# Attention with signed scale in the queries, its output split where it is copied, scores two pairs ahead, and a rebuilt seam between two model blocks

## The reference, cut to what matters

```python
def chunk_causal_attention(q, k, v, scale):          # head size 96 for q and k, 64 for v
    ...
        s = jnp.einsum('bqhd,bkhd->bhqk', qi, k).astype(jnp.float32) * scale
        s = jnp.where(mask[None, None], s, NEG)
        p = jax.nn.softmax(s, axis=-1).astype(v.dtype)
        return jnp.einsum('bhqk,bkhd->bqhd', p, v)
...
    y_a = jnp.einsum('bse,ed->bsd', o_a.reshape(b, s, MLA_HEADS * MLA_V), w_o_a)
    o_b = indexed_sparse_attention(q_b, k_b, v_b, q_i, k_i, w_i * (IDX_HEADS ** -0.5), top_k)
    y_b = jnp.einsum('bse,ed->bsd', o_b.reshape(b, s, DSA_HEADS * DSA_HEAD_DIM), w_o_b)
```

```python
    return x + m.reshape(b, s, d)                     # end of the first block: m is the experts' output
    x = rmsnorm(x, final_norm_g)
    h = layer_norm(jnp.concatenate([meta, x], axis=1), ln_in_g, ln_in_b)   # 16 meta tokens in front
    p = h @ w_in[l]                                   # second block; its first columns are conv_in
```

## Time and profile before

| | us |
|---|---|
| median of 3 runs | 2207.22 (2206.83 to 2208.47) |
| the profiled execution | 2207.27, span 2205.5 |
| attention (`attend`), first scores to last value product | 307.9 to 421.75 |
| wait of PE up to the projection's first matmul | to 426.98 |
| seam: last matmul of the experts to first of conv_in | 869.9 to 910.72 |
| PE busy | 1984.2 (90% of the span) |
| DVE, ACT, POOL busy | 1306.4, 938.7, 708.1 |

### The profile page before, as it was taken

The page is one execution under the profiler, slowest core; times in us unless marked ns, Lnnn a source line. Parts: engine busy times, 40 slices in busy tenths (PEclk is TensorE's granted clock), DMA queues, the critical chain, the costliest instruction groups (busy, mean ns, idle before and its releaser), DMA issues. The chain is left out here.

```text
span 2205.5 us, 36863 instructions
## 1 busy us (share of the span) xinstructions
PE 1984.2 (90%) x14734; PEld 1680.3 (76%) x14734; DVE 1306.4 (59%) x1946; ACT 938.7 (43%) x1485; POOL 708.1 (32%) x378
## 2 busy tenths in 40 slices
PE   7999998799799997598999796688899979999997
PEld 4777744475687876598999576687689979999784
DVE  2769645541789897505999565566431167887402
ACT  4324248623688887522222543234333143333312
POOL 3433300141011111143443164321035425555441
PEclk9999989999799999699999898799789999999999
DMA  4222210021999998223223013210132212232221
GB/s 177 96 67 94 69 48 1 23 89 70 362 358 373 369 371 317 79 88 119 92 87 136 29 43 106 44 31 15 40 116 87 87 48 96 87 97 92 81 96 38
DMA packets 89378, 260.09 MB, mean 118 GB/s; under 512 B 26304, under 2 KB 27472, under 8 KB 88464
## 3 DMA queue, kind: packets, MB, share of 16 engines
q1 hardware_dynamic: 85488, 247.90, 31.9%
q0 software_dynamic: 3744, 10.11, 1.3%
HBM read 239.10 MB, written 18.87 MB: 117 GB/s over the span
## 5 line engine op out<-in xcount | busy, mean ns | idle before, releaser
L1546 DVE TENSOR_TENSOR moe_wlo<-moe_ring,moe_whi 128x1024 fp32r<-128x1024 f32 x198 | 233.0, 1221 | 39.9 <-ACT moe_whi L1542 39.0
L537 PE MATMUL acc<-h_xhi,h_whi 128*128 128x264 f32 x816 | 234.4, 287 | 13.3 <-DVE h_xlo L463 7.4
L537 PE MATMUL acc<-h_xlo,h_whi 128*128 128x264 f32 x816 | 233.4, 286 | 0.0
L537 PE MATMUL acc<-h_xhi,h_wlo 128*128 128x264 f32 x816 | 233.1, 286 | 0.0
L1542 ACT ACTIVATE moe_whi<-moe_ring 128x1024 fp32r<-128x1024 f32 x198 | 206.0, 1059 | 40.6 <-PE acc L1602 22.6
L537 PE MATMUL acc<-ff_xhi,ff_whi 128*128 128x258 f32 x704 | 200.9, 285 | 9.3 <-DVE ff_xlo L463 9.3
L537 PE MATMUL acc<-ff_xhi,ff_wlo 128*128 128x258 f32 x704 | 199.8, 284 | 0.0
L537 PE MATMUL acc<-ff_xlo,ff_whi 128*128 128x258 f32 x704 | 199.7, 284 | 0.0
L395 POOL TENSOR_TENSOR h_wlo<-ring,h_whi 128x1024 fp32r<-128x1024 f32 x49 | 117.5, 2400 | 201.4 <-ACT h_whi L387 201.4
L537 PEld LDWEIGHTS acc<-h_xhi,h_whi 128*128 128x128 f32 x816 | 155.9, 191 | 14.5 <-DVE h_xlo L463 8.5
L1987 DVE SCALAR_TENSOR_TENSOR acc<-cp,par,acc 128x528 f32<-128x528 f32 x232 | 159.2, 765 | 0.0
(11 more groups left out here) (506 smaller groups left out, 5131.6 us busy)
## 6 DMA issues: line engine op xcount, KB each, us to landing
ring<-slabs SPq DMA_DIRECT2D x213, 512.0 KB, 3.5
moe_ring<-moe_slabs SPq DMA_DIRECT2D x204, 512.0 KB, 6.1
tok_rows<-h_tok SPq DMA_DIRECT2D x5, 512.0 KB, 4.2
h_spill<-x2r SPq DMA_DIRECT2D x1, 2112.0 KB, 6.6
v_spill<-rw_v SPq DMA_DIRECT2D x1, 2112.0 KB, 7.4
y_spill<-cp SPq DMA_DIRECT2D x8, 264.0 KB, 4.5
rw_v<-v_spill SPq DMA_DIRECT2D x1, 2112.0 KB, 8.0
x2r<-h_spill SPq DMA_DIRECT2D x1, 2112.0 KB, 8.5
```

Of the source, the lines that this page charges most:

```text
L537: mm = nc.tensor.matmul(acc[j][0:rows, s, 0:t1 - t0], wp[:, at:at + rows], xp[:, t0:t1], start=(k == 0 and m == 0), stop=(k == kt - 1 and ...
L1546: tensor_tensor(wlo[u % AHEAD][:, :], ringm[u % RAW][:, :], whi[u % AHEAD][:, :].bitcast(F32), ALU.subtract).then_inc(w_lo[u % 2], 1)
```

## The change

In attention: the scale moves, with a minus sign, into the copies that make the queries; masks are positive instead of negative; DVE keeps the minimum, which is the exponential's bias as it stands (scale -1), so L1284 is gone. The two output copies become one of 128x128, which writes the rounded half straight into the projection's operand; DVE writes the rest from PSUM in a new step (`low`); the next stage has no roundings and rests of its own. `att_sc` has three buffers, scores and masks run two pairs ahead, and DVE scales p before it masks p+2.

In the seam: meta rows and gain are loaded during the experts' stage; ACT and POOL split conv_in's first two slabs during the seam, not ACT and DVE behind it; the product with the gain goes to a buffer of its own (`y`), so it doesn't wait for the sum of squares; only the small eps term (`easing`) waits.

```diff
-                            nc.scalar.activation(dests[i], acc[i % 4][0:rows, 0, :], ACT.Copy).then_inc(tile_out, 1)
+                            nc.scalar.activation(dests[i], acc[i % 4][0:rows, 0, :], ACT.Copy,
+                                                 scale=-HD ** -0.5 if KR < i <= KR + 4 else 1.0).then_inc(tile_out, 1)
...
-                sc = [[sbt(ax, f"att_sc{i}{h_}", [P, T1]) for h_ in two] for i in two]
+                sc = [[sbt(ax, f"att_sc{i}{h_}", [P, T1]) for h_ in two] for i in range(3)]
...
                     scores(0)
+                    scores(1)
                     for p in range(NP + 1):
-                        if p + 1 < NP:
-                            scores(p + 1)
+                        if p + 2 < NP:
+                            scores(p + 2)
                         if p >= 1:
                             values(p - 1)
                         if p < NP:
...
-                            nc.vector.tensor_tensor_reduce(scr(p, h_), sbank(p, h_), bias(pairs[p][1]), 1.0, -3e38,
-                                                           ALU.add, ALU.max, one(mx, p, h_)).then_inc(s_out, 1)
+                            nc.vector.tensor_tensor_reduce(scr(p, h_), sbank(p, h_), bias(pairs[p][1]), 1.0, 3e38,
+                                                           ALU.add, ALU.min, one(mn, p, h_)).then_inc(s_out, 1)
...
+                    def low(p):
+                        o = pairs[p][0][4]
+                        dve.wait_ge(o_hi, p + 1)
+                        nc.vector.tensor_tensor(to(p, o.lo), obank(p), to(p, o.hi).bitcast(F32), ALU.subtract).then_inc(o_lo, 1)
+
                     add_bias(0)
+                    add_bias(1)
                     for p in range(NP):
-                        if p + 1 < NP:
-                            add_bias(p + 1)
                         normal(p)
+                        if p + 2 < NP:
+                            add_bias(p + 2)
+                        if p >= 2:
+                            low(p - 2)
+                    low(NP - 2)
+                    low(NP - 1)
...
                             act.wait_ge(s_out, 2 * p + h_ + 1)
-                            link("act", act, nc.scalar.activation(one(nm, p, h_), one(mx, p, h_), ACT.Copy, scale=-scale))
-                            nc.scalar.activation(scr(p, h_), scr(p, h_), ACT.Exp, bias=one(nm, p, h_),
-                                                 scale=scale, accum_out=one(rs, p, h_)).then_inc(probs, 1)
+                            nc.scalar.activation(scr(p, h_), scr(p, h_), ACT.Exp, bias=one(mn, p, h_),
+                                                 scale=-1.0, accum_out=one(rs, p, h_)).then_inc(probs, 1)
...
-                    def store(p):
-                        o, qt, i = pairs[p][0][5], pairs[p][1], pairs[p][2]
-                        for h_ in two:
-                            act.wait_ge(o_ready, 2 * p + 2)
-                            nc.scalar.activation(o[64 * h_:64 * h_ + 64, i, qt * P:(qt + 1) * P], obank(p, h_),
-                                                 ACT.Copy).then_inc(o_out, 1)
+                    def high(p):
+                        act.wait_ge(o_ready, p + 1)
+                        nc.scalar.activation(to(p, pairs[p][0][4].hi), obank(p), ACT.Copy).then_inc(o_hi, 1)
...
-                    w.begin(act, ["w_o_a"], ax, bx)
...
-                    ax.dve(dve)
-                    bx.dve(dve)
...
+                def for_seam(sp):
+                    sp.dma_start(gain, final_row.to_broadcast([P, D])).then_inc(gain_in, 16)
+                    sp.dma_start(xm, meta_rows).then_inc(meta_in, 16)
...
                     nc.clear_and_free_semaphores(first_sems)
+                    for n in first_slabs:
+                        w.pool(pool, n)
...
                     nc.scalar.activation(dummy[:, :], k0("eps", 1, EPS_RMS), ACT.Sqrt)
+                    for n in first_slabs:
+                        w.act(act, n)
                     act.wait_ge(m_centred, 1)
...
                         v.tensor_tensor(x[t][:, :], x[t][:, :], x1[:, t, :], ALU.add).then_inc(added, 1)
+                        dve.wait_ge(added, t + 1)
+                        L(v.tensor_tensor_reduce(y[t][:, :], x[t][:, :], gain, 1.0, 0.0, ALU.mult, ALU.add, one(total, t)))
+                        v.tensor_scalar(one(minus, t), one(total, t), -1.0 / D, None, ALU.mult).then_inc(gained, 1)
+
+                    def easing(t):
                         dve.wait_ge(squared, t + 1)
-                        L(v.tensor_tensor_reduce(x[t][:, :], x[t][:, :], gain[:, :], 1.0, 0.0, ALU.mult, ALU.add, one(total, t)))
...
-                        w.act(act, first_slabs[0])
                         nc.scalar.activation(hx.hi[:, :, 0:META], h[:, :, 0:META], ACT.Copy).then_inc(meta_hi, 1)
-                        for q in range(4):
-                            round_turned(q)
-                        w.act(act, first_slabs[1])
-                        for q in range(4, KD):
+                        for q in range(KD):
                             round_turned(q)
...
-                        w.dve(dve, first_slabs[0])
...
-                            if q == 4:
-                                w.dve(dve, first_slabs[1])
```

140 lines of the change are left out of this document (74 added, 66 removed).

## The result

The changed kernel takes **2158.16 us** (median of 4 runs, 2157.65 to 2159.13), the kernel before 2207.02 on the same chip (2199.84 to 2208.47). The ratio is 0.9781, with a 95% interval of 0.9764 to 0.9798: 48.9 us less.

The account below looks back on a forecast made before the run. The prediction took the attention to be bound by a once-a-round ring set by queue order, with no engine full. Terms of 20.9, 4.5 and 6.6 sum to 32.0 us off 2207.27: 2175.3, forecast 2175, range 2164 to 2190.

Parts of the forecast that it names:

- term 1: Attention: cutting the ring leaves the engine with most work setting each round; 93.0 us against 113.85, 20.9 less.
- two half-clock stretches: Attention: PE at half clock again at the start and later, each shorter, costing about 4 and 2.5 us.
- the start has nearly the same wait: Attention start: PE waits nearly as long as before, so half clock returns there; ten us of it cost about 4.
- a rival of 0.12: Attention: no half clock at all, 6.5 us less and the seam's 1.4, total 2167; chance 0.12.
- the ring: Attention: transposes, scores, masks and scaling follow each other once a round, 4.31 us at 512 keys of the second kind.
- Term 2: Hand-over from attention to projection: first matmul 3.6 us behind ACT's slab copy, 2.9 less, plus 1.6 of clock: 4.5 less.
- Term 3: Seam and behind it: adds 3.6 us apart, net 2.45, and 4.3 behind the seam: 6.6 us less.
- The 0.3 us by which POOL or DVE comes first: Seam: POOL's second split starts 0.3 us before DVE's meta-row scaling, which waits; the first add is 1.4 us later.
- The low clock: Rival, attention: half clock lasts as long as now, 20 and 7 us; total 2181; chance 0.2.
- Hand-offs: Rival, attention: ACT, DVE and PE nearly equal at 512 keys, so waits cost 0.3 a round, 9.6 us: 2185; chance 0.18.
- the ring isn't cut: Rival, attention: masks still wait for buffers or banks, only the borders gain: 2196; chance 0.02.
- POOL didn't hold the last rest: Judges the rival at both borders: POOL holds the last rest (2.3 us) and the seam's first add (2.3): 2180; chance 0.1.

Follow-up runs that it names:

- only the ring back: Changed kernel with attention order and depth as before (masks ahead of scaling, one pair ahead, two score buffers): 2191.75 us.
- after at half clock: Changed kernel with the seam undone (first two conv_in slabs split in the next stage again), same attention; profiled execution had half clock: median 2162.1 us.
- after run again: The changed kernel itself, unchanged, with five more executions: 2158.52 us.
- faster version: Changed kernel with the projection's first slab copied and split at pair 14, and the seam's second slab copy and POOL split later: 2147.75 us.
- the seam alone: Changed kernel with only the seam's part of the faster version (second slab copied behind the meta rows' root, POOL's second split later): 2160.06 us.

## Why the prediction was wrong in size

**The mechanism of term 1 held, two sizes didn't.** The attention gave 34.7 us and not 20.9. The missing 13.8 are three pieces. Those of the rounds are in every trace of after's attention; that of the clock is in part luck.

*The clock, 6.5.* I had charged two half-clock stretches, 4 us at the start and 2.5 behind it; the profiled execution had none. The second stretch is gone by the change: from 340 to the end of the attention all ten traces with the scaling ahead of the masks are at full clock, and all four with the masks first have one (PEclk of 366 to 386: 0.83, 0.61, 0.77, 0.66). The first is in part luck: with after's own wait it came in two traces of six. The price itself was right: where it did come, it cost 5.9 us for 13.7 us of half clock, against my 4 for ten. What failed is the step "the start has nearly the same wait": PE waited 2.29 us there before and 0.53 after. I counted the third set of scores as evidence only for a rival of 0.12 and didn't work out what it does to the wait: 0.66 us of work (1.79 against 1.13) more, and 1.09 less until the transposes start, since the 128x1 operations no longer stand ahead of the first exponentials (with them back, the transposes started 3.41 us behind the first scores, as before; with only the ring back, 2.32, as in after).

*The rounds, 6.3.* By groups of four pairs (transposes to transposes, in us; the last group three rounds):

| keys, kind | before | forecast | after | after at half clock |
|---|---|---|---|---|
| 128, first | 12.3 | 7.3 | 6.3 | 11.1 |
| 256, first | 14.4 | 8.9 | 9.4 | 10.5 |
| 384, first | 15.4 | 12.0 | 12.9 | 12.9 |
| 512, first | 14.8 | 16.0 | 12.3 | 12.3 |
| 128, second | 10.0 | 7.3 | 5.5 | 5.5 |
| 256, second | 13.2 | 8.9 | 8.1 | 8.1 |
| 384, second | 15.4 | 10.6 | 10.5 | 10.5 |
| 512, second | 12.0 | 9.3 | 8.8 | 8.8 |

Two steps are mis-sized. The rounds at 512 keys of the first kind were put at 3.99, with their own scores of 1.81 in each. Two pairs ahead, three of the four rounds of that group carry scores of the next one, which has 128 keys: they took 2.85, bound by the ring of transposes, copy and values, and the heavy scores stand in rounds at 384 keys (3.33 each instead of 3.0) that paid less for them. That group gave 3.6 us over the forecast; the two groups at 256 and 384 keys of the first kind gave 1.4 less than it. A round has to be added up from what stands in it after the change, not from the work of its own pair. My own table should have warned me: 16.0 is more than the 14.8 of before. The second is at 128 keys, 2.8 us in the two groups. I put these rounds at DVE's sum, 1.82; they took 1.5 to 1.6 in the first kind and 1.4 to 1.5 in the second, though PE, ACT and DVE are all nearly full there (timeline of after, a stretch of ACT and one of DVE):

```profile
312.59 0.44 ACT L1322 ACTIVATE att_pt<-acc 128x128 f32<-128x128 f32 x2
...
312.91 0.41 ACT L1314 ACTIVATE att_sc<-att_sc,att_mn 128x128 f32<-128x128 f32 x1
...
313.29 0.41 ACT L1314 ACTIVATE att_sc<-att_sc,att_mn 128x128 f32<-128x128 f32 x1
```
```profile
352.60 0.29 DVE L1284 CUSTOM_DVE_ANT_0 att_sc<-acc,c 128x128 f32<-128x128 f32 x1 [0.68 <-PE acc L1241]
...
353.62 0.16 DVE L1290 RECIPROCAL att_ri<-att_rs 128x1 f32<-128x1 f32 x1
353.81 0.29 DVE L1291 TENSOR_SCALAR att_sc<-att_sc,att_ri 128x128 f32<-128x128 f32 x1
...
354.05 0.42 DVE L1284 CUSTOM_DVE_ANT_0 att_sc<-acc,sel 128x256 f32<-128x256 f32 x1
```

Two copies take 0.44 together, not 0.54, and the next exponential starts 0.38 behind the last, though each is 0.41 long and has a reading of 0.19 behind it: instructions that follow each other on ACT overlap here by about 0.1 us. On DVE the nine instructions from 352.60 on add up to 1.90 us, and the next round's first starts 1.45 behind. (For ACT I had left out the two readings of 0.19 a round; its sum of 1.61 came out right at 128 keys of the first kind because the overlap made up for them.) A sum of mean durations was here an upper end of DVE's round; the distance from start to start is the size to add up.

*The start, 1.0:* transposes begin 2.3 us behind the first scores; I had put 3.2 there (the trace of before has 3.41), and the end took 2.9 of 3.0.

**Term 2** was about right in the profiled execution: 2.96 of 2.9 for the hand-over (3.53 of 3.6 from the slab copy), and 1.1 of 1.6 for the clock, whose low stretch comes earlier and is shorter, as 390 to 394 shows. But this part varies too: in the trace of after run again the clock is low from about 388 to 395 (in after for 3.4 us between 390 and 394), and the rounding of the gated sum comes 113.6 us behind the first scores instead of 112.5, so that nothing of the 1.6 came back there.

**Term 3** gave 8.1 of 6.6. Adds 3.6 apart (849.71, 853.28, 856.85) and the first at 883.55 by before's time (forecast 884.2) give 3.3 of 2.45; none of the last rests met a split (0.7 each, where the last took 2.87 before), and the way behind the seam gave 4.8 of 4.3. The 0.3 us by which POOL or DVE comes first fell as forecast; what it cost was measured from the other side, 3.1 us together with ACT's copies ahead of the square. Between the last rest and the end another 2.8 us appeared, for which I named nothing. 1.2 of them lie before the first sigmoid; the rest is in unchanged stages, whose length differs from trace to trace by some us.

**The rivals.** The low clock neither lasted nor came in the profiled execution; in those where it came it lasted 13 to 14 us, not 20. Hand-offs didn't eat the balance: PE waits 0.74 a round for one, but in rounds I had put at 3.1. That the ring isn't cut needed the masks to stay first, and the kernel that does just that lands at 2190. The nearest, no half clock, named 2167; it was mis-sized by the same rounds. POOL didn't hold the last rest (0.29), and what it held in the seam didn't delay the first add beyond the forecast. The range could have held the time only if its lower end had taken the rival of the clock together with the rounds as they came out.

## What to carry to other kernels

When every engine waits once a round, look for the in-order queue in which an instruction that could run stands behind one that can't. Moving it kept 25 of the 33.6 us that the cut was worth here, the deeper buffer alone nothing, and small instructions on another engine were worth little until the ring was cut. And a short idle time of PE between stages costs more than itself when the clock falls behind it: an early slab took 1.2 us off such a gap, and in its one trace the clock stayed full.

## What the runs showed of the hardware that I had not expected

The granted clock isn't a function of the kernel alone. Two executions of the same attention, with the same 0.5 us of waiting at its start, ran it at full and at half clock (PEclk 1.00 and 0.69 from 308 to 330), 5.9 us apart. With a wait of 0.79 us or more there the clock was low in seven traces of seven, with 0.53 us in two of six, and filling 1.91 of 2.29 us moved the fall by 4 us.

POOL's splits hold DVE instructions with a single input. The scaling of 16x1024 took 0.80 alone, 1.29 and 2.64 beside a split; one of 128x128 took 0.77 instead of 0.28. In the faster version's pair 14 two masks and a rest with an input in PSUM ran beside the split at 0.29 each, as elsewhere.

Where the faster version's last 3 us (5 between the two traces) are, behind the first sigmoid where no instruction differs, stays open. The stages from there to the end took 1271 us in its trace, 1275 and 1276 in the two of after, 1269 in the one with the seam undone and 1281 in the seam alone; their low-clock stretches between 1240 and 1560 differ from trace to trace.
